# A decoder layer on one core: a seventh feed-forward unit computed during the page loads

## The chip, the cores and the metric

The kernel runs on one core of one Trainium2 chip. TensorE (PE) does the products, VectorE (DVE), ScalarE (ACT) and GpSimd (POOL) the elementwise work, and SyncE (SP) issues nearly all DMAs. The metric is the device time of one execution in microseconds, as the median of several runs.

## The reference, cut to what matters

One decoder layer, float32, for a prompt of 256 tokens and eight samples of one token each, with 2048 earlier tokens per sample in a paged cache.

```python
z = x @ w_in                                  # q, k, v, B, C, h
att = attend(q, k, v)                         # 8 heads x 64; samples: block-sparse over cached pages
conv_y, conv_buf_new = causal_dwconv(gc * h, conv_buf, w_conv)
mix = jnp.concatenate([att, gb * conv_y], axis=-1) @ w_out
x1 = layer_norm(DEEPNORM_ALPHA * x + mix, ln1_g, ln1_b)
up, ffn_buf_new = causal_dwconv(x1 @ w_up, ffn_buf, w_fconv)     # w_up: 1024 x 5632
a, g = jnp.split(up, 2, axis=-1)
f = (jax.nn.silu(a) * g) @ w_down                                # w_down: 2816 x 1024
y = layer_norm(DEEPNORM_ALPHA * x1 + f, ln2_g, ln2_b)
```

## The kernel before, in words

Activations stand transposed: channels on the 128 partitions, and 264 columns (256 prompt tokens, then 8 samples). The feed-forward width of 2816 is cut into 22 units. A unit is 128 columns of the `a` half and 128 of the `g` half of `w_up`: 1 MB of weights, eight steps over the 1024 channels for each half.

The work comes in stages. First the input projection (`z_tile`) while the keys of all pages are scanned on VectorE, GpSimd and ScalarE (`multiply`, `reduce`, `multiply_page`, `sum_products`). Then the values: 32 groups of four pages (1 MB each, four DMAs), `values(b, s)` with number v = 4b + s, loaded by SyncE into a ring of homes (`HOMES`); from group 9 on, group v takes the home of group v - 6 and its load waits for that one's use (`s_vused`). Sample b is done after group 4b + 3: VectorE masks it (`masked_values`), PE transposes it (`sample_outputs`), VectorE sums the columns (`sample_columns`).

The first E = 6 units are *early*. Their weights are loaded among the values and PE multiplies them with the 256 prompt columns of `x1T` in plain float32 (`early_part`, `early_half(u, a)`), each unit in PSUM bank u % 4, between value groups. Units 0 to 3 come in four "quads" (rows of 512 columns, loaded by `load_quad`), units 4 and 5 as a pair for each half (rows of 256 columns, `load_pair`, behind groups 24 and 31), into the first half of the ring `wring`. ScalarE takes an early unit out of PSUM (`early_scaled`), VectorE convolves it (`early_convolved`), ScalarE applies silu, VectorE multiplies the halves (`gated`) into `fe`.

Where PE would stand idle among the last groups, `keep_clock(bank, n)` issues a product whose result nobody reads. Behind group 31 PE does the samples' path: their rows of the mixer output, the layer norm, and then, once the samples' `x1` is there (`s_xsp`), the product of the samples with all early units' weights. For it the kernel uses strips of 32 PE columns, four at once: the two halves of two units form one group, and there are ES = 3 groups, each with its PSUM bank; ScalarE copies a group's result (`ev`), and PE transposes it. GpSimd splits `x1` meanwhile into a high and a low part.

Then the *late* units, NL = 16 of them: ScalarE rounds the weights to a high part (`up_high`), VectorE subtracts (`low`), and PE does three products per step over all 264 columns (`split_product`, high times high, high times low, low times high), alternating between two slots (`late_slot`) with two PSUM banks each. SyncE loads a late unit (`load_up`, two DMAs with rows of 128 columns) once the slot is free. The down product follows in the same manner, eight tiles of 22 steps (`down_tile`), then the second layer norm.

The orders in each engine's queue are written out by hand; engines meet at semaphores only. The query buffer `qk[:, 0]` (4096 columns) holds the broadcast queries until the key scan ends; its first half takes quad 0 after sample 3's keys, and `qk[:, 1]` holds products of the scan, and `fe` later. The last product of the key scan is well ahead of value group 20.

Of the kernel before, what the change touches and what calls it, by code (L numbers as in the profile page):

```python
# [22 lines left out]
P = 128  # L23
D = 1024
KT = D // P
# [23 lines left out]
E = 6  # L49
QUAD = 4  # L50
ES = E // 2
# [8 lines left out]
def build(nc, x_prompt, x_sample, cache_k, cache_v, state_conv, state_ffn_conv, page_table,  # L60
# [13 lines left out]
    with ctx:  # L74
# [98 lines left out]
        quads = [h.rearrange("p (k n) -> p k n", k=KT // 2) for h in quad_home]  # L173
        pairs = [wring[:, 0, a * UNIT:(a + 1) * UNIT].rearrange("p (k n) -> p k n", k=KT) for a in range(2)]

        def early(u, k, a):
            if u < QUAD:
                return quads[2 * a + k // 4][:, k % 4, u * P:(u + 1) * P]
            return pairs[a][:, k, (u - QUAD) * P:(u - QUAD + 1) * P]

        fe = qk[:, 1, 0:E * NPR].rearrange("p (u n) -> p u n", u=E)
# [23 lines left out]
                     (NS, ps[0:NS, 2:4, :], NPR, srows[0:NS, :]))  # L205
# [116 lines left out]
        def down_bank(m):  # L322
            return 7 if m == 0 else m % 2
# [14 lines left out]
        def _(sp):  # L338
# [77 lines left out]

            def load_pair(a):
                sp.wait_ge(s_mix, KT)
                first = a * FF + QUAD * P
                sp.dma_start(pairs[a], wup[:, :, first:first + 2 * P]).then_inc(s_eu[4 + a], 16)  # L420
# [45 lines left out]
            for b in range(3, NS):  # L466
                ids_v = page_ids(b)
                for s in range(SLOTS):
                    v = SLOTS * b + s
                    load_values(v, ids_v)  # L470
                    if v in (12, 13):
                        load_quad(v - 10)
                    elif v in (24, 31):
                        load_pair((24, 31).index(v))
# [162 lines left out]
        def _(act):  # L637
# [177 lines left out]
            def early_scaled(u):  # L815
                bank = ps[:, u % 4, :].rearrange("p (a n) -> p a n", a=2)
                act.wait_ge(s_u, QUAD + 1 + u if u < QUAD else 2 * QUAD + 3 + u - QUAD)
# [23 lines left out]
            for u in range(QUAD):  # L841
                early_scaled(u)
                silu(u)
# [4 lines left out]
            early_scaled(4)  # L848
            early_scaled(5)
            silu(4)  # L850
            silu(5)
            act.wait_ge(s_sr, 1)
            for i in range(ES):
                act.wait_ge(s_es, i + 1)
                nc.scalar.activation(ev[:, i, :], ps[:, (7, 4, 5, 6)[i], 0:P], ACT.Copy).then_inc(s_ec, 1)
# [44 lines left out]
        def _(dve):  # L900
# [305 lines left out]
            sample_columns(5)  # L1206
            masked_values(6)
            sample_columns(6)
# [30 lines left out]
            early_convolved(4)  # L1239
            early_convolved(5)  # L1240
            gated(4)
            gated(5)
            low(1, UNIT)
# [120 lines left out]
        def _(pe):  # L1364
# [329 lines left out]
            def early_part(u, a, first, end):  # L1694
                if first == 0:
                    if u == QUAD:
                        pe.wait_ge(s_eu[4 + a], 16)
                    elif u == 0:
                        pe.wait_ge(s_eu[2 * a], 16)
                    if a == 0 and u >= 4:  # L1700
                        pe.wait_ge(s_cv, 2 * (u - 4) + 2)
                        pe.wait_ge(s_tl, u - 3)
# [42 lines left out]
            value_range(21, 23)  # L1745
            sample_outputs(3)
            early_half(3, 1)
            value_range(23, 25)
            sample_outputs(4)
            early_half(4, 0)  # L1750
            value_range(25, 27)
            sample_outputs(5)
            early_half(5, 0)
            value_range(27, 30)
            sample_outputs(6)
            pe.wait_ge(s_cv, 2 * QUAD)
            pe.wait_ge(s_tl, QUAD)
            keep_clock(3, 448)
            value_range(30, 31)
            keep_clock(3, 512)  # L1760
            keep_clock(3, 384)
# [3 lines left out]
            early_part(4, 1, 0, 4)  # L1765
# [11 lines left out]
            early_part(4, 1, 4, KT)  # L1777
# [4 lines left out]
            early_half(5, 1)  # L1782
# [5 lines left out]
            for i in range(ES):  # L1788
                units = range(2 * i, 2 * i + 2)
# [7 lines left out]
            for i in range(ES):  # L1797
                pe.wait_ge(s_ec, i + 1)
                turn(ps[:, 7, i * P:(i + 1) * P], ev[:, i, :]).then_inc(s_et, 1)
# [129 lines left out]
```

## Time and profile before

| | |
|---|---|
| median of 3 runs | 447.43 us (447.05 to 448.56) |
| the profiled execution | 448.32 us |
| its span, first to last instruction | 446.5 us |
| PE busy | 416.1 us (93%), 2911 products |
| VectorE busy | 296.0 us (66%) |
| ScalarE busy | 181.6 us (41%) |
| GpSimd busy | 104.4 us (23%) |
| moved by DMA | 124.85 MB, mean 280 GB/s |
| chain that ended last | PE 55%, VectorE 18%, SyncE's queue 11%, issue 6%, DMA 5% |

The span is what the profile's times count from; the execution's own time has about 1.8 us more around it. Busy times of PE overlap from one product to the next, since products are pipelined: the time from start to start is what a product costs, and it is shorter than its duration. A float32 product appears as two instructions.

### The profile page before, as it was taken

How to read it: one execution, taken by the hardware profiler on the slowest of the kernel's cores; microseconds unless marked ns; L12 is line 12 of the kernel's file. 1: busy time of each engine (PE TensorE's matmuls, PEld its weight loads, DVE VectorE, ACT ScalarE, POOL GpSimd, SP SyncE). 2: the span in 40 equal slices, each digit the busy share in tenths (PEclk: the TensorE clock that was granted, in tenths of full speed). 3: DMA queues.
4: the chain of work that ended last, by engine and by line, in shares of the span. 5: the costliest groups of instructions: out<-in, count | busy, mean ns of one | idle time of the engine just before them, and what ended most of it. 6: DMA issues, size and time to landing. Idle time of an engine off the chain costs nothing.

```text
span 446.5 us, 8259 instructions
## 1 busy us (share of the span) xinstructions
PE 416.1 (93%) x2911; PEld 341.0 (76%) x2911; DVE 296.0 (66%) x383; ACT 181.6 (41%) x694; POOL 104.4 (23%) x133
## 2 busy tenths in 40 slices
PE   4999999999999998999798989999999999999990
PEld 4588887876866774664364369999999999999990
DVE  0496999999799976944351264766666877534536
ACT  1476568653377334011110043455554456224201
POOL 1003033995255231100000436211222221000002
PEclk9999999999999999999999999999999999999997
DMA  8999999999999999999999953566666685968002
GB/s 294 385 329 386 385 388 379 370 357 390 398 386 372 351 393 387 386 386 386 386 377 386 304 166 111 159 178 189 189 182 170 166 215 155 234 174 212 24 1 97
DMA packets 109515, 124.85 MB, mean 280 GB/s; under 512 B 5775, under 2 KB 66920, under 8 KB 109466
## 3 DMA queue, kind: packets, MB, share of 16 engines
q1 hardware_dynamic: 101138, 107.55, 72.5%
q10 hardware_dynamic: 8336, 16.78, 10.5%
q8 instruction: 23, 0.38, 0.4%
q14 instruction: 18, 0.15, 0.1%
HBM read 121.90 MB, written 2.61 MB: 279 GB/s over the span
## 4 chain that ended last, share of the span: by engine, by line
PE 55%; DVE 18%; SPq 11%; issue 6%; DMA 5%; POOL 2%; ACT 1%; DVEq 0%; POOLq 0%; ACTq 0%
PE ps L1815 11%; PE ps L1816 11%; PE ps L1817 11%; SPq L354 8%; DVE qk L930 5%; DVE T L940 5%; PE ps L1432 4%; PE ps L1627 4%; PE ps L1708 3%; PE ps L1603 3%; PE ps L1629 3%; PE ps L1372 3%; DMA wring<-in_cache_v 2%; DMA KV<-in_cache_k 2%; POOL x1l L605 1%
## 5 line engine op out<-in xcount | busy, mean ns | idle before, releaser
L1177 DVE TENSOR_TENSOR wlo<-KV,whi 128x2048 fp32r<-128x2048 f32 (+1 forms) x24 | 61.8, 2576 | 57.1 <-ACT whi L832 29.1
L1432 PE MATMUL ps<-xT,wring 128*128 128x264 f32 x384 | 89.6, 389 | 0.0
L1432 PEld LDWEIGHTS ps<-xT,wring 128*128 128x128 f32 x384 | 71.9, 191 | 13.4 <-issue 1.7
L1815 PE MATMUL ps<-x1h,whi 128*128 128x264 f32 x256 | 73.8, 288 | 0.2
L930 DVE TENSOR_TENSOR qk<-KV,qk 128x1536 f32<-128x1536 f32 (+1 forms) x32 | 67.8, 2122 | 9.2 <-DMA KV<-in_cache_k 5.5
L1817 PE MATMUL ps<-x1h,wlo 128*128 128x264 f32 x256 | 72.7, 284 | 0.0
L1816 PE MATMUL ps<-x1l,whi 128*128 128x264 f32 x256 | 72.7, 284 | 0.0
L662 ACT ACTIVATE qk<-qk 128x64 f32<-128x64 f32 x216 | 51.8, 244 | 28.5 <-POOL qk L553 21.1
L940 DVE TENSOR_REDUCE T<-qk 128x24 f32<-128x1536 f32 (+1 forms) x32 | 58.4, 1827 | 0.0
L1815 PE MATMUL ps<-fh,whi 128*128 128x264 f32 x176 | 50.4, 286 | 0.1
L1816 PE MATMUL ps<-fl,whi 128*128 128x264 f32 x176 | 50.0, 284 | 0.0
L1817 PE MATMUL ps<-fh,wlo 128*128 128x264 f32 x176 | 50.0, 284 | 0.0
L1815 PEld LDWEIGHTS ps<-x1h,whi 128*128 128x128 f32 x256 | 48.3, 189 | 1.6 <-issue 1.4
L1816 PEld LDWEIGHTS ps<-x1l,whi 128*128 128x128 f32 x256 | 48.3, 189 | 0.0
L1817 PEld LDWEIGHTS ps<-x1h,wlo 128*128 128x128 f32 x256 | 48.1, 188 | 0.0
L832 ACT ACTIVATE whi<-KV 128x2048 fp32r<-128x2048 f32 x16 | 30.6, 1915 | 42.3 <-PE ps L1817 42.3
L662 ACT ACTIVATION_READ_ACCUMULATOR qk<-qk 128x1 f32 x216 | 41.0, 190 | 0.0
L553 POOL TENSOR_TENSOR qk<-KV,qk 128x512 f32<-128x512 f32 x19 | 28.9, 1525 | 45.7 <-DMA KV<-in_cache_k 24.0
L1157 DVE SCALAR_TENSOR_TENSOR U<-ps,stT,U 128x255 f32<-128x255 f32 (+1 forms) x84 | 34.5, 474 | 0.0
L1815 PEld LDWEIGHTS ps<-fh,whi 128*128 128x128 f32 x176 | 33.2, 189 | 0.5 <-DVE wlo L1177 0.4
L1816 PEld LDWEIGHTS ps<-fl,whi 128*128 128x128 f32 x176 | 33.2, 189 | 0.0
L1817 PEld LDWEIGHTS ps<-fh,wlo 128*128 128x128 f32 x176 | 33.1, 188 | 0.0
(218 smaller groups left out, 578.9 us busy)
## 6 DMA issues: line engine op xcount, KB each, us to landing
KV<-in_cache_k SPq DMA_DIRECT2D x128, 256.0 KB, 7.3
KV<-in_w_ffn_up SPq DMA_DIRECT2D x32, 512.0 KB, 5.1
KV<-in_cache_v SPq DMA_DIRECT2D x60, 256.0 KB, 8.5
wring<-in_cache_v SPq DMA_DIRECT2D x56, 256.0 KB, 7.5
KV<-in_w_ffn_down SPq DMA_DIRECT2D x8, 1408.0 KB, 7.0
wring<-in_w_in ACTq DMA_DIRECT2D x5, 2048.0 KB, 15.1
zbuf<-in_cache_v SPq DMA_DIRECT2D x12, 256.0 KB, 6.0
zbuf<-in_w_ffn_up SPq DMA_DIRECT2D x3, 1024.0 KB, 11.5
```

Source lines behind the costliest of these rows:

```text
L354: sp.dma_start(dst[:, g, :], pages[bass.ds(ids[g], 1)].rearrange("o t d -> (o t) d")).then_inc(landed, 16)
L553: nc.gpsimd.tensor_tensor(prod[:, j % 2, GD * DA:GP * DA], kv[:, s, GD, :], qb[:, b, :], ALU.mult).then_inc(s_kpool, 1)
L662: ins = nc.scalar.activation(x, x, ACT.Copy, accum_out=T[:, b // 4, GP * s + GD, b % 4 * NH + h:b % 4 * NH + h + 1])
L832: nc.scalar.activation(whi[s][:, 0:UNIT], w2[s][:, 0:UNIT], ACT.Copy).then_inc(s_hi, 1)
L930: nc.vector.tensor_tensor(prod[:, j % 2, 0:n * DA].rearrange("p (g d) -> p g d", g=n), kv[:, s, 0:n], q, ALU.mult).then_inc(s_kused, 1)
L940: nc.vector.tensor_reduce(dst, prod[:, j % 2, 0:n * DA].rearrange("p (g h d) -> p g h d", h=NH, d=DH), AX.X, ALU.add).then_inc(s_red, 1)
L1157: nc.vector.scalar_tensor_tensor(out, bank[:, 0:n], tap(u + a * FT, k), out, ALU.mult, ALU.add)\
L1177: nc.vector.tensor_tensor(wlo[s][:, 0:n], w2[s][:, 0:n], whi[s][:, 0:n], ALU.subtract).then_inc(s_lo, 1)
L1432: ins = nc.tensor.matmul(ps[:, z_bank(n), 0:R], tile[k], xT[:, k, :], start=k == 0, stop=k == KT - 1)
L1815: nc.tensor.matmul(out, wh[k], xh[k], start=k == 0, stop=False)
L1816: nc.tensor.matmul(out, wh[k], xl[k], start=False, stop=False)
L1817: ins = nc.tensor.matmul(out, wl[k], xh[k], start=False, stop=k == n - 1)
```

## The change

E goes from 6 to 7, so there are 15 late units, and ES from 3 to 4 groups, of which the last holds one unit (two strips). The new fifth unit (u = 4, "solo") gets the second half of the query buffer. SyncE loads it behind value group 20 in two DMAs, with rows of 128 columns. The pairs, loaded where they were, now hold units 5 and 6. PE does both halves of unit 4 around value group 23, the first halves of 5 and 6 behind groups 25 and 26 to 27, and the second halves of 5 and 6 where those of 4 and 5 were. Of the four unread products (448, 512, 384 and 320 columns) those of 448 and 384 go. Convolution and gating of unit 4 go ahead in VectorE's and ScalarE's queues. As NL is odd now, the down product begins in the other slot, and its PSUM banks and those of the last rows change with it.

```diff
--- before.py
+++ after.py
@@ -46,9 +46,9 @@
 Z_ORDER = (0, 1, 4, 5, 2, 3)
 STATE_ROWS = 2 * NS
 STACK = STATE_ROWS + 3
-E = 6
+E = 7
 QUAD = 4
-ES = E // 2
+ES = (E + 1) // 2
 NL = FT - E
 WHOLE = (14, 16, 18, 20, 31)
 POOLED = (9, 10, 11, 12) + tuple(range(17, 32))
@@ -171,13 +171,17 @@
         UNIT = KT * 2 * P
         quad_home = [qk[:, 0, 0:UNIT], zbuf[:, UNIT:2 * UNIT], zbuf[:, 2 * UNIT:3 * UNIT], zbuf[:, 0:UNIT]]
         quads = [h.rearrange("p (k n) -> p k n", k=KT // 2) for h in quad_home]
+        solo = qk[:, 0, UNIT:2 * UNIT].rearrange("p (k a n) -> p k a n", k=KT, a=2)
         pairs = [wring[:, 0, a * UNIT:(a + 1) * UNIT].rearrange("p (k n) -> p k n", k=KT) for a in range(2)]
 
         def early(u, k, a):
             if u < QUAD:
                 return quads[2 * a + k // 4][:, k % 4, u * P:(u + 1) * P]
-            return pairs[a][:, k, (u - QUAD) * P:(u - QUAD + 1) * P]
-
+            if u == QUAD:
+                return solo[:, k, a, :]
+            return pairs[a][:, k, (u - QUAD - 1) * P:(u - QUAD) * P]
+
+        assert E * NPR <= 2 * UNIT - KT * R
         fe = qk[:, 1, 0:E * NPR].rearrange("p (u n) -> p u n", u=E)
         w2 = [KV[:, s * FT * P:(s + 1) * FT * P] for s in range(2)]
         U = at("U", hs_mem, [P, 2, 2, NPR], F32)
@@ -202,7 +206,7 @@
         ps = ctx.enter_context(nc.psum_tensor("ps", [P, 8, 512], F32))[:]
 
         row_tiles = ((P, ps[:, 4:6, :], 0, rows[:, 0, :]), (P, ps[:, 6:8, :], P, rows[:, 1, :]),
-                     (NS, ps[0:NS, 2:4, :], NPR, srows[0:NS, :]))
+                     (NS, ps[0:NS, 0:2, :], NPR, srows[0:NS, :]))
         first_rows = ((P, ps[:, 2:4, :], 0, rows[:, 0, :]), (P, ps[:, 0:2, :], P, rows[:, 1, :]),
                       (NS, ps[0:NS, 4:6, :], NPR, srows[0:NS, :]))
 
@@ -320,7 +324,7 @@
             return (0, 1, 4)[m % 3]
 
         def down_bank(m):
-            return 7 if m == 0 else m % 2
+            return 7 if m == 0 else 2 * late_slot(NL) + m % 2
 
         def act_sums(j):
             return sum(i not in WHOLE for i in range(j))
@@ -414,9 +418,15 @@
                     sp.wait_ge(s_vused, 7)
                 sp.dma_start(quads[i], wup[:, k:k + 4, a * FF:a * FF + QUAD * P]).then_inc(s_eu[i], 16)
 
+            def load_solo():
+                sp.wait_ge(s_kused, NS * SLOTS)
+                sp.wait_ge(s_kpool, pool_pages(NS * SLOTS))
+                for a in range(2):
+                    sp.dma_start(solo[:, :, a, :], wup[:, :, QUAD * P + a * FF:QUAD * P + a * FF + P]).then_inc(s_eu[6], 16)
+
             def load_pair(a):
                 sp.wait_ge(s_mix, KT)
-                first = a * FF + QUAD * P
+                first = a * FF + (QUAD + 1) * P
                 sp.dma_start(pairs[a], wup[:, :, first:first + 2 * P]).then_inc(s_eu[4 + a], 16)
 
             load_consts(0, 8)
@@ -470,6 +480,8 @@
                     load_values(v, ids_v)
                     if v in (12, 13):
                         load_quad(v - 10)
+                    elif v == 20:
+                        load_solo()
                     elif v in (24, 31):
                         load_pair((24, 31).index(v))
             sp.wait_ge(s_ctail, 1)
@@ -814,7 +826,7 @@
 
             def early_scaled(u):
                 bank = ps[:, u % 4, :].rearrange("p (a n) -> p a n", a=2)
-                act.wait_ge(s_u, QUAD + 1 + u if u < QUAD else 2 * QUAD + 3 + u - QUAD)
+                act.wait_ge(s_u, QUAD + 1 + u if u < QUAD else 2 * QUAD + 2 if u == QUAD else 2 * QUAD + 4 + u - QUAD)
                 if u >= 2:
                     act.wait_ge(s_f, u - 1)
                 for a in range(2):
@@ -838,21 +850,22 @@
 
             exponentials(1)
             nc.scalar.activation(idle, nhalf[:, 0:1], ACT.Silu)
-            for u in range(QUAD):
+            for u in range(QUAD + 1):
                 early_scaled(u)
                 silu(u)
             act.wait_ge(s_sw, 1)
             nc.scalar.activation(er[:, 0, :], ps[:, 6, :], ACT.Copy).then_inc(s_swc, 1)
             up_high(0)
             normalise(first_rows, 2, s_shift, 2, s_srx)
-            early_scaled(4)
             early_scaled(5)
-            silu(4)
+            early_scaled(6)
             silu(5)
+            silu(6)
             act.wait_ge(s_sr, 1)
             for i in range(ES):
                 act.wait_ge(s_es, i + 1)
-                nc.scalar.activation(ev[:, i, :], ps[:, (7, 4, 5, 6)[i], 0:P], ACT.Copy).then_inc(s_ec, 1)
+                n = P if 2 * i + 1 < E else P // 2
+                nc.scalar.activation(ev[0:n, i, :], ps[0:n, (7, 4, 5, 6)[i], 0:P], ACT.Copy).then_inc(s_ec, 1)
             up_high(1)
 
             def late_scaled(v):
@@ -1204,7 +1217,9 @@
             early_convolved(3)
             gated(3)
             sample_columns(5)
+            early_convolved(4)
             masked_values(6)
+            gated(4)
             sample_columns(6)
             masked_values(7)
             sample_columns(7)
@@ -1236,10 +1251,10 @@
             nc.vector.tensor_copy(x1h[:, :, NPR:R], new).then_inc(s_xsh, 1)
             dve.wait_ge(s_xsh, 1)
             nc.vector.tensor_tensor(x1l[:, :, NPR:R], new, x1h[:, :, NPR:R], ALU.subtract).then_inc(s_xsh, 1)
-            early_convolved(4)
             early_convolved(5)
-            gated(4)
+            early_convolved(6)
             gated(5)
+            gated(6)
             low(1, UNIT)
             dve.wait_ge(s_et, ES)
             tails = uptail[:, 2:NTAIL, :].rearrange("p r (a n) -> p a n r", a=2)
@@ -1694,6 +1709,8 @@
             def early_part(u, a, first, end):
                 if first == 0:
                     if u == QUAD:
+                        pe.wait_ge(s_eu[6], 32)
+                    elif u == QUAD + 1:
                         pe.wait_ge(s_eu[4 + a], 16)
                     elif u == 0:
                         pe.wait_ge(s_eu[2 * a], 16)
@@ -1742,27 +1759,32 @@
             sample_outputs(2)
             value_range(20, 21)
             early_half(2, 1)
-            value_range(21, 23)
+            value_range(21, 22)
+            early_half(3, 1)
+            value_range(22, 23)
             sample_outputs(3)
-            early_half(3, 1)
-            value_range(23, 25)
+            early_half(4, 0)
+            value_range(23, 24)
+            early_half(4, 1)
+            value_range(24, 25)
             sample_outputs(4)
-            early_half(4, 0)
-            value_range(25, 27)
+            value_range(25, 26)
+            early_half(5, 0)
+            value_range(26, 27)
             sample_outputs(5)
-            early_half(5, 0)
-            value_range(27, 30)
+            early_part(6, 0, 0, 4)
+            value_range(27, 28)
+            early_part(6, 0, 4, KT)
+            value_range(28, 30)
             sample_outputs(6)
+            value_range(30, 31)
             pe.wait_ge(s_cv, 2 * QUAD)
             pe.wait_ge(s_tl, QUAD)
-            keep_clock(3, 448)
-            value_range(30, 31)
             keep_clock(3, 512)
-            keep_clock(3, 384)
             value_range(31, 32)
             keep_clock(3, 320)
             sample_outputs(7)
-            early_part(4, 1, 0, 4)
+            early_part(5, 1, 0, 4)
             pe.wait_ge(s_xso, 1)
             pe.wait_ge(s_om, NS)
             for c in range(2):
@@ -1774,19 +1796,19 @@
                 ins = nc.tensor.matmul(ps[32 * g:32 * g + NS, 6 + m // 4, g * P:(g + 1) * P], rT[:, m, NPR:R], ident,
                                        start=False, stop=True)
             ins.then_inc(s_sw, 1)
-            early_part(4, 1, 4, KT)
+            early_part(5, 1, 4, KT)
             pe.wait_ge(s_swc, 2)
             for c in range(2):
                 ins = nc.tensor.matmul(ps[0:NS, 4 + c, :], sel, er[:, c, :], start=True, stop=True)
             ins.then_inc(s_sr, 1)
-            early_half(5, 1)
+            early_half(6, 1)
             pe.wait_ge(s_srx, 1)
             for m in range(KT):
                 ins = turn(ps[:, 6, 256 + m * NS:256 + (m + 1) * NS], srows[0:NS, m * P:(m + 1) * P], NS)
             ins.then_inc(s_sb, 1)
             pe.wait_ge(s_xsp, 1)
             for i in range(ES):
-                units = range(2 * i, 2 * i + 2)
+                units = range(2 * i, min(2 * i + 2, E))
                 for k in range(KT):
                     for u in units:
                         for a in range(2):
@@ -1796,7 +1818,8 @@
                 ins.then_inc(s_es, 1)
             for i in range(ES):
                 pe.wait_ge(s_ec, i + 1)
-                turn(ps[:, 7, i * P:(i + 1) * P], ev[:, i, :]).then_inc(s_et, 1)
+                n = P if 2 * i + 1 < E else P // 2
+                turn(ps[:, 7, i * P:i * P + n], ev[0:n, i, :], n).then_inc(s_et, 1)
 
             def split_product(out, wh, wl, xh, xl, prompt=None, between=None):
                 n = len(wh)
```

## Rows read from the trace of the kernel before

**Rows 1.** The page: three rows of the span in 40 slices.

```profile
PE   4999999999999998999798989999999999999990
...
DMA  8999999999999999999999953566666685968002
GB/s 294 385 329 386 385 388 379 370 357 390 398 386 372 351 393 387 386 386 386 386 377 386 304 166 111 159 178 189 189 182 170 166 215 155 234 174 212 24 1 97
```

**Rows 2.** Windows: engines' busy time (instructions), granted clock, DMA share, GB/s.

```profile
243.00:245.00 2.00, 0.92 (x8) 0.16 (x8) 0.00 (x0) 0.00 (x0) 0.00 (x0) 1.00 1.05 386
...
251.00:253.00 2.00, 1.38 (x8) 0.79 (x7) 1.22 (x3) 0.00 (x0) 1.84 (x4) 1.00 1.06 274
```

**Rows 3.** Timeline of PE, 216 to 253 us: start, duration, instruction, idle before.

```profile
216.81 1.07 PE L1603 MATMUL ps<-KV,Pw 128*32 128x512 f32 x8 [1.83 <-DMA KV<-in_cache_v]
217.81 3.72 PE L1708 MATMUL ps<-catT,zbuf 128*128 128x256 f32 x16
221.46 1.07 PE L1603 MATMUL ps<-KV,Pw 128*32 128x512 f32 x8
222.34 1.04 PE L1603 MATMUL ps<-wring,Pw 128*32 128x512 f32 x8
223.31 0.66 PE L1372 MATMUL ps<-ident,OM 128*128 128x128 f32 x4
223.81 3.62 PE L1708 MATMUL ps<-catT,zbuf 128*128 128x256 f32 x16
227.36 1.07 PE L1603 MATMUL ps<-KV,Pw 128*32 128x512 f32 x8
...
246.79 1.07 PE L1603 MATMUL ps<-wring,Pw 128*32 128x512 f32 x8 [0.30 <-DMA wring<-in_cache_v]
247.79 1.77 PE L1645 MATMUL ps<-diag,ident 128*128 128x512 f32 x4
249.53 1.06 PE L1603 MATMUL ps<-KV,Pw 128*32 128x512 f32 x8
...
251.41 0.66 PE L1372 MATMUL ps<-ident,OM 128*128 128x128 f32 x4
252.61 2.00 PE L1708 MATMUL ps<-catT,wring 128*128 128x256 f32 x8 [0.54 <-DMA wring<-in_w_ffn_up]
```

**Rows 4.** Timeline of SyncE's queue: the issue of value group 30.

```profile
235.24 2.19 SPq L354 DMA_DIRECT2D wring<-in_cache_v  x4
```

**Rows 5.** Chain of waits, and timeline of PE: the samples' up product.

```profile
266.05 5.45 PE ps L1794 x192
...
266.05 0.30 PE L1794 MATMUL ps<-qk,xsP 128*32 128x128 f32 x1 [0.94 <-DVE xsP L1235]
266.06 0.30 PE L1794 MATMUL ps<-zbuf,xsP 128*32 128x128 f32 x1
...
266.19 0.27 PE L1794 MATMUL ps<-qk,xsP 128*32 128x128 f32 x1
```

**Rows 6.** Chain of waits: late units 0 and 14; and a window over all 16.

```profile
272.23 0.35 PE ps L1815
...
355.68 0.35 PE ps L1815
...
272.20:367.30 95.10, 94.93 (x768) 93.60 (x768) 65.70 (x92) 48.25 (x91) 23.63 (x39) 1.00 0.64 175
```

**Rows 7.** Windows: one late unit's load each, and one half microsecond.

```profile
278.00:281.00 3.00, 3.00 (x28) 3.00 (x27) 0.76 (x1) 2.70 (x5) 2.51 (x5) 1.00 1.08 300
...
290.00:293.00 3.00, 3.00 (x27) 3.00 (x26) 1.11 (x2) 2.83 (x6) 0.00 (x0) 1.00 1.10 307
...
291.50:292.00 0.50, 0.50 (x7) 0.50 (x6) 0.00 (x0) 0.50 (x2) 0.00 (x0) 1.00 1.15 346
```

**Rows 8.** Timeline of VectorE: convolution and gating of early unit 3.

```profile
230.51 1.64 DVE L1157 SCALAR_TENSOR_TENSOR U<-ps,stT,U 128x255 f32<-128x255 f32 x4
232.26 0.43 DVE L1172 TENSOR_TENSOR qk<-U 128x256 f32<-128x256 f32 x1
```

## The prediction

> **What bounds the kernel now.** I read the page first, for which resource is full where. The slices of the span [rows 1] show two regimes. Up to the 24th slice (about 257 us) DMA is at 9 tenths and moves some 386 GB/s; after it TensorE (PE) is at 9 tenths in every slice and DMA is not. So a microsecond of PE work costs one only behind about 250 us, and a megabyte costs time only before it. The change takes an FFN unit out of the second regime and puts it into the first.
>
> Next the stretches of the span by window [rows 2], to see whether the first regime is full to its end. It is: at 243 us the share of the DMA engines is 1.05, with 386 GB/s, the level of the slices before. The order of PE's work between 216 and 253 us [rows 3] shows that PE follows the transfers: value groups 20 and 30, and behind them the half on the second pair, each start behind an idle time that a DMA ends. From the start of group 20 (216.81) to that of group 30 (246.79) eleven megabytes land (groups 21 to 30 and one pair): 29.98 / 11 = 2.73 us each. SyncE's issues [rows 4] run far ahead of that: group 30 is issued at 235.24 and used 11.55 us later, so its queue always has work.
>
> Then the chain of waits for the two stretches behind: the sample rows' up product of the early units [rows 5] and the late units [rows 6]. The chain enters the first late unit at 272.23 and the fifteenth at 355.68, 14 units on: 83.45 / 14 = 5.96 us each, and there PE has no gap to speak of (94.93 us busy of 95.10). The granted clock is 1.00 (2.4 GHz) in every stretch read.
>
> **The change part by part.**
>
> *One late unit fewer.* It removes 48 products of the split kind: 5.96 us of PE, all on the path. The transition to the down product is reached by the same orders in every queue; slots and PSUM banks only swap parity. **-5.96 us.** ScalarE, VectorE and GpSimd lose or move their share of that unit, which PE hides.
>
> *The load of the solo unit.* 1 MB more before the end of the value phase, two DMAs behind group 20. SyncE does not wait for it: group 14 already needed the same count of used keys. Its two issues stand in a queue that is 11.55 us ahead. The price is transfer time, since DMA is full. At the rate of the other megabytes it is 2.73 us. But this one has rows of 128 columns, as the late units' loads have, and these are slower [rows 7]: a late load fills the engines (share 1.08 and 1.10) at 300 and 307 GB/s, its best half microsecond is 346. 1.05 MB at 307 is 3.4 us. The lower bound is 2.73; the upper is 3.8, from the 274 GB/s of 251 to 253 us, where such a load goes beside other things [rows 2]. The late loads are the same kind, so I take **3.4 us**. The Trainium skill (DMA: Bandwidth & Descriptors, Specifications) says that transfers reach line rate from 512 bytes on, which is the length of these rows. By that rule the load would take the 2.73 us. The trace does not agree: 307 against 386 GB/s; the rule's result is a rival below.
>
> *PE's products in the value phase.* Two halves are added (before: two single halves of 4 and 5; after: both of 4, one each of 5 and 6), two unread products go. From [rows 3]: a half takes 3.65 us (217.81 to 221.46), later ones 3.55, say 3.6; a value group 0.95 (1.00, 0.88, 0.97); four transposes 0.5. Does PE still reach group 31 in time? In the new queue, group 21 lands at 216.8 + 3.4 + 2.7 = 222.9 and PE waits for it. Behind that, ahead of group 31, stand ten groups (9.5), five halves (18.0), four sets of transposes (2.0) and the one unread product left (0.9: half of the row of 1.77 for two): 30.4 us, so 253.3. Group 31 lands at about 246.8 + 2.7 + 3.4 = 252.9. PE is thus level with the transfers, 0.4 us behind: group 31 starts at 253.3, 3.8 us later than the 249.53 of before. Next late is the half that uses the second pair: the old one waited 0.54 us for its load and began at 252.61; the new one is released by the load at 252.61 + 3.4 = 256.0, or by PE at 251.9 + 3.8 = 255.7. So the load decides, and **what follows shifts by 3.4 us**, 3.3 to 3.8 as the two trade places. PE's lateness can also reach the loads, since group v + 6 waits for the home of v. The narrowest: group 24 is used by 237.9, and SyncE would issue group 30 at 235.24 + 3.4 = 238.6. Even a miss of some microseconds is covered by the 11 us that are in the queue.
>
> *VectorE and ScalarE.* Convolution and gating of unit 4 (1.64 + 0.43 us [rows 8]) move ahead of masked_values(6) and sample_columns(6); behind them wait sample_outputs(6), value group 30's successors and the tail. The fifth sample's transposes end near 244.4, its column sum at 245.1, the convolution at 246.8; the mask waits for group 27 (about 247.1) and is done at 247.9, and PE wants it at 250.9. Three microseconds of cover, so nothing; without cover it would be 2.1 us at most. The tail keeps two units (5, 6 for 4, 5) and is as long as before.
>
> *The sample rows' product.* Three groups of two units take 5.45 us, 1.82 each [rows 5]. The new fourth holds one unit, so two column strips of PE instead of four. Within a group the four strips start together (266.05, 266.06) and the next four instructions follow a pass later (266.19), and so on, so a strip's own pass sets the time and half a group costs a whole one: **+1.8 us**; if it were set by the count of instructions, 0.9, the lower bound. Above 1.82 nothing points. The copy of its result and the transposes behind it follow the last group as before, and nothing new is exposed.
>
> **Sum:** -5.96 + 3.4 + 1.8 = -0.76 us. On the profiled execution: span 446.5 to 445.7, time 448.32 to 447.6. The median of the runs is 447.43, 0.9 below the profiled one, so I predict 447.43 - 0.76 = **446.7 us**. What a measurement can tell from no change is 0.3% or 1.34 us.
>
> **Rivals.**
>
> *A. The solo load goes at full rate.* Then it costs 2.73 us, but PE takes over as the bound: group 21 lands 0.7 earlier, PE reaches the half of the second pair at 255.0, against a load at 255.3, a shift of 2.7 to 3.1. That gives 2.9 + 1.8 - 5.96 = -1.3: 446.2 us, on the edge of faster. For it: half microseconds of 346 GB/s, and a queue that is never empty hides the ramps of a lone load. Against: 307 over a whole load at a share above the value phase's. The skill's rule named above would make this the outcome.
>
> *B. The fourth sample group costs half.* 3.4 + 0.9 - 5.96 = -1.7: 445.8 us, faster. With A as well it would be -2.2, 445.3. Against it: the even pace of the groups of four strips.
>
> *C. TensorE becomes the bound (the other side).* The place is the run of five halves ahead of group 31. The sum leaves PE 0.4 us behind the load. Every further microsecond there, by a wait of unit 6's first half for its bank or of sample_outputs(6) for the mask, goes one for one into the tail once the pair's load is passed (0.3 us). The change is level when the shift reaches 4.16 us (5.96 - 1.8), PE then 0.7 us later than summed; slower by 0.3% from 5.5 us on, PE 2.1 us later than summed. A VectorE chain that misses its 3 us of cover by 2 would do: 447.43 + 1.5 = 448.9 us. For it: only 0.9 us of unread products is left as cushion, and VectorE's queue has more in it; against: every wait that I followed has microseconds of room.
>
> *D. No net change of any kind,* the load at 3.8 us: 3.8 + 1.8 - 5.96 = -0.4, 447.1 us.
>
> **How the numbers follow.** The forecast (load 3.2 to 3.6, fourth group 1.8) 0.45; A 0.15; B 0.12, with or without A; C 0.13, about a quarter of it short of the 0.3% bound; D 0.15. Faster by over 0.3%: B, and half of A, and a little of the forecast by the scatter of medians (the runs of before span 447.05 to 448.56): 0.23. Slower: C's greater part and a trace of D: 0.12. Same: 0.65. The range: down to 445.6, B's value with some scatter; up to 448.2, between no change and C's 448.9, which leaves out about 0.1 on each side.
>
> **What the profile after should show.** The late units still 5.96 us apart, 15 of them; the first one entered at 272.23 + 3.4 + 1.8 = 277.4 us. The sample product at 7.2 to 7.3 us instead of 5.45, starting at 269.4. DMA's share still 1.05 to 1.1 through 250 us, with some 3 us of it at 300 to 340 GB/s between 217 and 224 us. Group 31 at 253 to 253.5 us with little or no idle time of PE in the ten groups before it; the solo's first half not waiting for its load. The mask of the seventh sample before 249 us. The prediction is wrong if the shift at the half of the second pair is under 2.9 or over 4 us, if the fourth sample group takes under 1.6 us, or if PE waits for VectorE between 244 and 252 us.

## The result, and the profile after

The kernel after takes **449.33 us** (median of 13 runs, 448.35 to 451.36) against 447.67 us for the kernel before beside it (13 runs): a ratio of 1.0034, 95% interval 1.002 to 1.0048. It is slower. The forecast was 446.7 us, with a range of 445.6 to 448.2.

The profiled execution took 448.92 us with a span of 447.1 us, 0.6 us over that of before. The page has the same two regimes as [rows 1]:

```profile
PE 418.0 (93%) x2924; PEld 341.5 (76%) x2924; DVE 294.5 (66%) x382; ACT 179.8 (40%) x693; POOL 104.7 (23%) x133
...
PE   5999998999999998998799997999999999999990
...
DMA  8999999999999999999999963366666685968002
...
q8 instruction: 23, 0.38, 0.4%
```

The last row played no part in the prediction: a DMA queue that carries instructions. In 23 packets it moves 16 KB each, in the kernel before too, and PE has 5,848 instruction records (2924 of products and as many of weight loads), one packet for some 254 of them. That the queue is PE's is inferred: the other engines have under 700 records each.

The chain of waits, from the samples' up product into the late units (start, duration, what), answers to [rows 5] and [rows 6]:

```profile
269.25 5.23 PE ps L1816 x184
274.48 1.64 issue
276.13 2.16 PE ps L1816 x40
278.29 0.68 PE ps L1387 x4
...
278.98 0.36 PE ps L1838
...
350.51 0.36 PE ps L1838
```

The product starts at 269.25, as expected (269.4). Then, after 184 of its 224 product records, PE stops for 1.64 us. The row says "issue": no semaphore and no transfer that the profile ties to an instruction. The first late unit starts at 278.98, 9.73 us behind the product's start; before it was 6.16 us by the timeline. The late units are 5.96 us apart as before (278.98 to 350.51, 12 units). So the block costs 3.57 us more, where 1.8 were in the sum.

The timeline of PE in the value phase (start, duration, instruction, idle before) answers to [rows 3]:

```profile
212.63 1.06 PE L1618 MATMUL ps<-KV,Pw 128*32 128x512 f32 x8 [1.44 <-DMA KV<-in_cache_v]
...
215.48 1.07 PE L1618 MATMUL ps<-KV,Pw 128*32 128x512 f32 x8 [1.19 <-DMA KV<-in_cache_v]
216.48 3.72 PE L1725 MATMUL ps<-catT,zbuf 128*128 128x256 f32 x16
221.91 1.06 PE L1618 MATMUL ps<-KV,Pw 128*32 128x512 f32 x8 [1.72 <-DMA KV<-in_cache_v]
...
252.14 1.13 PE L1660 MATMUL ps<-diag,ident 128*128 128x512 f32 x2
253.20 1.06 PE L1618 MATMUL ps<-KV,Pw 128*32 128x512 f32 x8
...
255.81 1.99 PE L1725 MATMUL ps<-catT,wring 128*128 128x256 f32 x8
```

The rows are groups 19, 20, the half between, 21, the one unread product, group 31 and the half on the second pair. Group 21 is the last that PE waits for; from 221.91 on its queue is full, and group 31 starts at 253.20 (forecast 253.3). The half on the second pair starts 3.20 us later than before; counted from group 19, the last one that the solo load can't touch, 43.18 us against 39.28 (252.61 - 213.33, a start that the trace of before gives), 3.9 us later. VectorE's mask of the seventh sample is done before 248 us, with the room that was forecast.

### The profile page after: what moved, and what is told of

It is laid out like the page before. It is cut to its first block, busy times and chain, and to the rows that moved or that the text cites. A ratio compares the mean times of both kernels' runs of the same rounds, so it can differ in the third digit from the quotient of the medians.

```text
span 447.1 us, 8281 instructions
## 1 busy us (share of the span) xinstructions
PE 418.0 (93%) x2924; PEld 341.5 (76%) x2924; DVE 294.5 (66%) x382; ACT 179.8 (40%) x693; POOL 104.7 (23%) x133
## 4 chain that ended last, share of the span: by engine, by line
PE 58%; DVE 18%; SPq 10%; issue 6%; DMA 4%; POOL 2%; ACT 1%; DVEq 0%; POOLq 0%; ACTq 0%
PE ps L1838 11%; PE ps L1839 10%; PE ps L1840 10%; PE ps L1725 6%; SPq L358 5%; DVE qk L943 5%; DVE T L953 5%; PE ps L1618 5%; PE ps L1447 4%; PE ps L1642 3%; PE ps L1644 3%; PE ps L1387 3%; DMA KV<-in_cache_k 2%; PE ps L1816 2%; POOL x1l L617 1%
## 5 line engine op out<-in xcount | busy, mean ns | idle before, releaser
L1190 DVE TENSOR_TENSOR wlo<-KV,whi 128x2048 fp32r<-128x2048 f32 (+1 forms) x23 | 59.5, 2588 | 58.7 <-ACT whi L844 31.0
L1838 PE MATMUL ps<-x1h,whi 128*128 128x264 f32 x240 | 68.9, 287 | 0.4
L1839 PE MATMUL ps<-x1l,whi 128*128 128x264 f32 x240 | 68.0, 283 | 0.0
L1840 PE MATMUL ps<-x1h,wlo 128*128 128x264 f32 x240 | 68.0, 283 | 0.0
L1838 PEld LDWEIGHTS ps<-x1h,whi 128*128 128x128 f32 x240 | 45.2, 188 | 1.7 <-issue 1.6
L1839 PEld LDWEIGHTS ps<-x1l,whi 128*128 128x128 f32 x240 | 45.3, 189 | 0.0
L1840 PEld LDWEIGHTS ps<-x1h,wlo 128*128 128x128 f32 x240 | 45.0, 188 | 0.0
L844 ACT ACTIVATE whi<-KV 128x2048 fp32r<-128x2048 f32 x15 | 28.7, 1915 | 39.5 <-PE ps L1840 39.5
L565 POOL TENSOR_TENSOR qk<-KV,qk 128x512 f32<-128x512 f32 x19 | 27.3, 1442 | 45.8 <-DMA KV<-in_cache_k 22.7
```

Of the source, the lines that this page charges most:

```text
L565: nc.gpsimd.tensor_tensor(prod[:, j % 2, GD * DA:GP * DA], kv[:, s, GD, :], qb[:, b, :], ALU.mult).then_inc(s_kpool, 1)
L844: nc.scalar.activation(whi[s][:, 0:UNIT], w2[s][:, 0:UNIT], ACT.Copy).then_inc(s_hi, 1)
L1190: nc.vector.tensor_tensor(wlo[s][:, 0:n], w2[s][:, 0:n], whi[s][:, 0:n], ALU.subtract).then_inc(s_lo, 1)
L1838: nc.tensor.matmul(out, wh[k], xh[k], start=k == 0, stop=False)
L1839: nc.tensor.matmul(out, wh[k], xl[k], start=False, stop=False)
L1840: ins = nc.tensor.matmul(out, wl[k], xh[k], start=False, stop=k == n - 1)
```

## The experiments

Three theories of the gap were put to the test. **I**: PE's instructions come in blocks by DMA, and where a block edge falls in the dense sample product decides. **C**: the block comes late because its transfer stands behind another load. **L**: the product is simply too long now. The windows show the other load. In the kernel after, the load of late unit 2 fills the engines until 274 us; the queues' rows of 271 to 273 us, and of 273 to 275 us, are

```profile
q1 hardware_dynamic: 1273, 0.64, 112.3%
```

```profile
q1 hardware_dynamic: 242, 0.12, 24.5%
q8 instruction: 1, 0.02, 3.7%
```

so the 16 KB go when the 1 MB is nearly through (at 273.58, 4.33 us into the product), and PE goes on at 276.13.

The kernel before has the same late packet: it too goes 4.33 us into the product, at 270.38, and PE does not stop there. What differs is the count of instructions ahead of the product. These rows of windows, from the span's start to the product's, are those of the kernel before, of the kernel after and of run 1 below; the third column is PE's busy time and its product records, each with a weight load beside it:

```profile
0.00:266.04 266.04, 246.56 (x1386) 1.00 1.02 365
0.00:269.24 269.24, 252.76 (x1414) 1.00 1.02 365
0.00:265.93 265.93, 249.32 (x1414) 0.99 1.02 365
```

The change puts 28 product records, so 56 instructions, ahead of the product: 64 for the two halves of one more unit, less 8 for the two dropped unread products. Run 1 puts the same 56 into the kernel before.

**1. The kernel before with 56 instructions more** ahead of the product, where PE waits for a transfer anyway.

```diff
+            def tiny(count):
+                pe.wait_ge(s_cv, 2)
+                pe.wait_ge(s_tl, 1)
+                for i in range(count):
+                    nc.tensor.matmul(ps[0:32, 0, 0:1], ident[:, 0:32], diag[:, 0:1], start=True, stop=True)
...
+            tiny(14)
             value_range(20, 21)
```

> The kernel before, with 14 one-column products that nobody reads (56 instructions of PE) in front of value group 20, where PE waits 1.83 us for a transfer anyway. Theory I (instruction blocks): PE's instructions arrive in blocks by DMA, and the 1.64 us gap of the kernel after lies where a block came late in the dense sample product; what matters is where the block edge falls, and 56 more instructions put it here as in the kernel after. Then a gap of about 1.3 to 1.7 us appears at instruction 350 or so of the sample product or just behind it, the first late unit starts at 273.5 to 274, and the time goes up by 1.3 to 1.7 us, to about 449.2. Theory L (length): the gap comes because the product has 224 instead of 192 instruction pairs. Then nothing changes: first late unit 6.2 us behind the product's start, time within 0.4 us of before. Theory N (the seventh unit itself: its buffer, its strips) also says no change.

Measured: 450.03 us against 447.46, ratio 1.0053 (1.0034 to 1.0073), more than the 1.3 to 1.7 us expected. The timeline of PE in the sample product:

```profile
270.33 0.84 PE L1801 MATMUL ps<-wring,xsP 128*32 128x128 f32 x24
272.79 0.43 PE L1801 MATMUL ps<-wring,xsP 128*32 128x128 f32 x8 [1.62 <-issue]
273.15 0.80 PE L1372 MATMUL ps<-ident,ev 128*128 128x128 f32 x3
273.93 0.36 PE L1822 MATMUL ps<-x1h,whi 128*128 128x264 f32 x1
```

Nothing of the change is in this kernel, and the gap is there, 1.62 us, behind the 184th product record as in the kernel after. Group 31 starts within 0.1 us of where it did (249.48). Theory L and the seventh unit as such fall. From the product's start to the first late unit it is 7.99 us, 1.83 more than before. The rest of the 2.6 us fits another cause: this profile has a stretch at half clock near 73 us, of which below, and five of the seven executions have a mean granted clock of 0.987 or 0.988 as it does; the other two took 449.04 and 449.84 us.

**2. and 3. The kernel after with 128 and with 64 instructions more**, half in front of group 20 and half in front of group 21. The edit is shown for 128; for 64 it has `tiny(8)` twice.

```diff
+            tiny(16)
             value_range(20, 21)
             early_half(2, 1)
+            tiny(16)
             value_range(21, 22)
```

> The kernel after, with 16 unread one-column products in front of value group 20 and 16 in front of group 21 (128 instructions of PE), where PE idles 1.19 and 1.72 us. Theory I: the block edge moves from inside the sample product to ahead of it, where PE's instructions are slow; the gap shrinks from 1.64 to under 0.6 us and the time falls by 1 to 2 us, to 447.3 to 448.3. Theory L and N: the gap stays at 1.6 us, time within 0.4 us of the kernel after (449.3).

> As the run with 128 instructions, but with 64 (8 and 8 products). Theory I: the block edge is still among the last instructions ahead of the product or its first, and the next block is needed inside it: the gap stays, 1.4 to 2 us, a little earlier in the product (near instruction 285 rather than 349). Theory L: the gap stays where it is. So together with the run with 128 it tells a place in the stream from a mere count of instructions added.

Measured: with 128, 447.60 us, ratio to before 1.0002 (0.9985 to 1.0018), no gap, first late unit 7.87 us behind the product's start. With 64, 448.78 us, ratio 1.0025 (1.0009 to 1.0041), a gap of 0.75 us, at 5.10 us into the product where it was at 6.88 us in the kernel after (the instruction behind the gap):

```profile
273.73 0.30 PE L1824 MATMUL ps<-wring,xsP 128*32 128x128 f32 x1 [0.75 <-issue]
```

The gap moves earlier and shrinks with more instructions put in front. With 64 it stands behind the 151st product record in place of the 184th, 66 instructions earlier (33 products and as many weight loads). I had expected 64 not to shrink it; the direction of the place was right, the size not. The trace shows why it shrank: the packet went 2.57 us into the product here, while the load of late unit 2 was still running. In all four profiles with a gap (the kernel after here and in run 10, runs 1 and 3) PE goes on 2.5 to 2.6 us behind the packet's start.

**4. The kernel after with the load of late unit 2 held** until the sample product is complete.

```diff
             for v in range(2, NL):
                 sp.wait_ge(s_lo, v - 1)
+                if v == 2:
+                    sp.wait_ge(s_es, ES)
                 load_up(v)
```

> The kernel after, with the load of late unit 2 held until the sample product is complete; unit 2 is not needed until 12 us later. Theory C (contention): the instruction block waits behind this load's packets, as its own transfer begins 4.3 us after the product's start in both traces, near the end of the load. Then the gap goes to under 0.5 us, and the time to 447.6 or so. If the block is late only for its position (theory I without contention) the gap stays at 1.6 us and the time at 449.3. If the load is held too long, the high part of unit 2 is late and PE waits there; expected 0.

Measured: 447.60 us against 447.46, ratio 0.9991 (0.9973 to 1.0009). The instruction stream of PE is that of the kernel after; the gap is gone. Its chain, and the queues' rows of 271 to 273 us:

```profile
269.86 7.18 PE ps L1818 x224
277.04 0.68 PE ps L1389 x4
277.73 0.36 PE ps L1840
```

```profile
q8 instruction: 1, 0.02, 3.0%
```

The packet now goes at 271.5, 1.7 us into the product, not 4.3.

**5. and 6. The kernel before with the hold**, with and without the 56 instructions.

> The kernel before with the 56 instructions of unread products, and the load of late unit 2 held until the sample product is complete. Theory I+C: the gap needs both, a block edge that falls badly and a load that the block's transfer stands behind. With the load held, the block's transfer begins some 1.7 us after the product's start instead of 4.3, the gap of 1.62 us goes, and the time is back within 0.4 us of before. Rival (position alone; the hold only helped the kernel after by chance): gap 1.6 us and 449.5 to 450.

> The kernel before with only the hold of that load. There is no gap in its trace, so the hold has nothing to remove: theory I+C says no change (within 0.4 us). Rival: the hold pays for another reason, for instance less traffic beside the sample product; then it gains 1 us or more here too, and its gain in the kernel after says nothing of instruction blocks.

Measured, against 447.17 us: 448.08 us with both (ratio 1.001, 0.9995 to 1.0026) and no gap, 6.16 us from the product's start to the first late unit as in the kernel before; 447.87 us with the hold alone (1.0017, 0.9999 to 1.0035). So the hold takes away what the 56 instructions cost, and gains nothing where there is no gap. The gap needs both: the edge in the wrong place and the load ahead of the block.

**7. The hold, and a half moved ahead of group 21**, into the wait of 1.72 us.

```diff
-            value_range(21, 22)
             early_half(3, 1)
+            value_range(21, 22)
```

> The kernel after with the hold, and the second half of early unit 3 moved ahead of value group 21, where PE waited 1.72 us for the transfer that the solo load had delayed. Theory T (the transfers bound the tail): PE reaches group 31 1.7 us earlier, finds it not landed, and the tail moves by 0.2 to 0.5 us only. Theory P (PE bounds the tail, its queue being full from group 21 on): the tail moves by 1 us or more, to under 446.8 us.

Measured: 447.61 us, ratio 1.0013 (0.999 to 1.0035), no gain that six runs can tell. Its trace has PE wait 0.59 us for group 31 (starting at 252.05) and 1.11 us for the second pair (255.69): the transfers bind. From group 19 to that half it is 42.75 us, 3.47 more than before. So theory T holds. The 3.47 us are the price of the solo load where nothing else binds; 3.4 was forecast.

**8. and 9. The hold, and the solo buffer from rows of 512 columns**, twice. The same 1 MB comes in longer rows, but they are other weights: these two kernels leave out the right values of unit 4 and serve for the time alone.

```diff
-                for a in range(2):
-                    sp.dma_start(solo[:, :, a, :], wup[:, :, QUAD * P + a * FF:QUAD * P + a * FF + P]).then_inc(s_eu[6], 16)
+                flat = qk[:, 0, UNIT:2 * UNIT].rearrange("p (k n) -> p k n", k=4)
+                for a in range(2):
+                    sp.dma_start(flat[:, 2 * a:2 * a + 2, :], wup[:, 2 * a:2 * a + 2, 0:512]).then_inc(s_eu[6], 16)
```

> The kernel after with the hold, and the solo buffer filled from rows of 512 columns (2 KB) in place of 128 (512 bytes), the same 1 MB; it holds other weights, so unit 4's values are not the reference's. Theory R (row length): group 21 lands 5.5 us behind group 20 instead of 6.3 or so, and the tail comes 0.6 to 0.9 us earlier, near 446.9. If row length does not matter for the time, as the rule of 512 bytes says, nothing changes (within 0.3 us).

> The solo buffer from rows of 2 KB once more. Its trace showed group 21 landing 8.80 us behind group 19, against 8.88 with the rows of 512 bytes: no gain; its median was 1.9 us lower. If the trace is right, the median comes within 0.5 us of the kernel with the held load beside it. If the median is right, it is again 1 us or more below.

Measured: ratios to before of 0.9974 (0.9953 to 0.9996) and 0.9978 (0.996 to 0.9997), against 0.9991 and 1.0001 for the hold alone: about 0.9 us, though the intervals overlap. From group 19 to group 21 the two traces have 8.80 and 8.10 us, those of the hold alone 8.88 and 8.85. Counted from group 20, which the solo load stands right behind, both show it: 5.31 and 5.18 us to group 21, against 5.96 and 5.90 with the hold alone and 6.43 in the kernel after. (Group 20 itself came 0.6 us later in run 8 than in the others, which hides it from group 19 on.) So long rows land some 0.7 us sooner at this place; that the whole kernel gains as much is likely by the times, not shown.

**10. and 11. The kernel after and the one with the hold once more**, beside each other.

> The kernel after once more, for its distribution and a second profile beside the same runs of before as the next three. Theory I+C: the gap is in this profile too, 1.5 to 1.9 us, at the same instruction of the sample product; time 1.2 to 1.8 us above before.

> The kernel after with the held load once more, to settle the size: the sum of the other terms (5.96 saved, 3.4 and 1.8 paid) says 0.8 us faster than before, 446.6 to 447; if the first measurement (level with before) stands, the paid terms come to 6 us rather than 5.2. Against the kernel after 1.5 to 2 us faster.

Measured, against 448.17 us: after 449.86 us, ratio 1.004 (1.002 to 1.006), with a gap of 1.74 us at the same instruction; with the hold 447.64 us, 1.0001 (0.9982 to 1.002), level again and not the 0.8 us faster that was expected. The profile of the first also shows the following around group 21, first the timeline of PE, then the windows (the third column from the right is the granted clock):

```profile
222.84 1.57 PE L1618 MATMUL ps<-KV,Pw 128*32 128x512 f32 x8 [1.98 <-DMA KV<-in_cache_v]
224.34 4.00 PE L1725 MATMUL ps<-catT,zbuf 128*128 128x256 f32 x12
```

```profile
221.00:223.00 2.00, 0.16 (x4) 0.16 (x8) 0.00 (x0) 0.80 (x3) 0.00 (x0) 1.00 1.04 376
223.00:225.00 2.00, 2.00 (x10) 0.57 (x3) 0.00 (x0) 0.00 (x0) 0.00 (x0) 0.57 1.05 392
225.00:227.00 2.00, 2.00 (x7) 1.62 (x6) 0.00 (x0) 0.00 (x0) 0.00 (x0) 0.58 1.04 385
```

Behind the wait for group 21, 1.98 us here, the clock falls to 1.2 GHz for about 3.4 us. As PE has no slack from there on, it arrives late: from group 19 to the sample product 58.28 us, in the first profile of the same kernel 56.62. Of these 1.7 us, 0.4 lie ahead of group 21, which came later itself; 1.3 lie behind it (48.64 us to the product against 47.34). It is in one profile of two.

**12. The hold, and one of eight steps of the fourth sample group**, so the kernel leaves out most of unit 6 for the samples.

```diff
-                for k in range(KT):
+                steps = KT if i < 3 else 1
+                for k in range(steps):
```

> The kernel after with the held load, and one of eight steps of the fourth sample group (unit 6's products with the samples over 128 of the 1024 channels only). Theory S (a strip's pass sets the pace, so half a group costs a whole one): the sample product is shorter by 7/8 of 1.82 = 1.6 us, and the time falls by as much, to 1.6 us below the run with the held load. Rival (the count of instructions sets it): 0.8 us.

Measured: ratio 0.9962 (0.9941 to 0.9982), 1.7 us below the hold alone; product and transposes 6.34 us instead of 7.87, so 1.5 us less where 1.6 was expected by theory S and 0.8 by its rival. Theory S holds.

**13. and 14. Versions meant to be kept**: the hold, with the fourth group on all four strips, and the same with the half moved as in 7. The edit is shown without the hold and without the wider copy and transpose of the group.

```diff
-                            g = 32 * (2 * (u % 2) + a)
+                            g = 32 * (2 * ((u if i < 3 else k) % 2) + a)
                             ins = nc.tensor.matmul(ps[g:g + 32, (7, 4, 5, 6)[i], 0:P], xsP[:, k, :], early(u, k, a),
-                                                   start=k == 0, stop=k == KT - 1)
+                                                   start=k < (1 if i < 3 else 2), stop=k >= (KT - 1 if i < 3 else KT - 2))
...
+            chain(ins)
+            for a in range(2):
+                src = ps[:, 7, :].rearrange("p (n a x) -> p a n x", a=2, x=32)
+                ins = nc.vector.tensor_tensor(tails[:, a, E - 1:E, :], tails[:, a, E - 1:E, :], src[:, a, E:E + 1, 0:NS], ALU.add)
             ins.then_inc(s_ett, 1)
```

> The kernel after with the held load, and the fourth sample group spread over all four strips: unit 6's even steps on strips 0 and 1, odd steps on strips 2 and 3, the two halves added on the way out. Theory S (a strip's pass sets the pace): the group takes 0.9 instead of 1.8 us, the sample product with its transposes 7.0 instead of 7.87, and the time is 0.9 us below the kernel with the held load: 446.6 to 447, 0.2 to 0.3% under before. Rival (instructions set the pace): 7.87 stays and the time is level with before.

> The same with the second half of early unit 3 ahead of value group 21, as in the earlier run, whose trace had PE wait for group 31 and the second pair instead (transfers bind there): nothing more than 0.3 us under the run beside it. If the gap between the spans (0.6 to 0.9 us below before) and the medians (level) comes from PE's full queue among the groups, which a stretch at half clock then hits in full, this one with its spare 0.6 and 1.1 us of PE should be 0.5 us better in the mean.

Measured: 447.33 us, ratio 0.9982 (0.9964 to 0.9999), and 446.32 us, ratio **0.9965** (0.9951 to 0.998). The chain of the first:

```profile
268.83 6.32 PE ps L1822 x224
275.15 0.72 PE ps L1393 x4
275.88 0.35 PE ps L1844
```

Product and transposes take 7.05 us instead of 7.87, as expected; the time is 0.3 us above the 446.6 to 447 expected. The second is faster than both kernels of this study: 0.35% under before. That it is also faster than the first (0.9982) the overlapping intervals do not show.

## Why the prediction was wrong

**The step that failed** is the last of *The sample rows' product*: "Above 1.82 nothing points", and "nothing new is exposed". The group itself costs what was said: with the gap away, product and transposes are 7.87 us, 1.71 over 6.16 (forecast 1.8). What the step put at nothing is a wait for PE's own instructions, 1.64 and 1.74 us in the two profiles; with it the block is 9.73 and 9.82 us long, 1.9 us over 7.87. This is the densest stretch of the kernel: 224 product records and as many weight loads in 7.2 us, so the 254 instructions of a block last some 4.1 us there against 15 us in the late units (two in 0.12 us). The gap needs two things. One is the place of the block's edge: the change puts 56 more instructions ahead of the product, and run 1 shows that these 56 alone bring the gap, at the same record, without the seventh unit and its longer product. The other is that the block's transfer goes late beside the load of late unit 2, which SyncE issues as soon as `low(0)` is done, 0.65 us ahead of the product, in both kernels. Runs 2, 4 and 5 take away one of the two each, the edge's place (2) or the load (4, 5), and the gap goes. Whether the longer product would have met an edge without the shift was not run. Why PE goes on only some 1.4 us after the packet's end stays open as well.

The Trainium skill (Runtime: NRT & Kernel Launch, Instruction fetch mechanics) describes this fetch, in blocks of 16 KiB by a DMA queue of the sequencer, and calls its cost mostly hidden; the block size agrees with the 23 packets here, the "hidden" does not, with 1.64 us on the path.

**Late unit, -5.96:** right; 5.96 from unit to unit again.

**Solo load, +3.4:** right, 3.47 where only the transfers bind. The row that was used for it (307 GB/s for rows of 128 columns) decided well against the 2.73 us of the full rate. Rival A did not come about. The landing of group 21 behind group 20 says the same by another row: 6.43 us for two megabytes where the full rate would give 5.5, and 5.2 to 5.3 once the rows were long.

**PE's products in the value phase:** right in the sum (group 31 at 253.20, forecast 253.3) and in the verdict that PE and the transfers are level. In the profile the half on the second pair came 3.9 us later counted from group 19, just above the 3.3 to 3.8 given (counted from the span's start 3.20, just below); with the hold the sample product is 3.4 and 3.5 us later counted in the same way. The 1.72 us wait at group 21 was in my sum ("PE waits for it"), but not what it can do: in one profile of two the clock fell behind it, and 1.3 us were lost.

**VectorE and ScalarE, 0:** right; the mask is done 2.9 us ahead of its use.

**The sum.** Counted from group 19, the traces give -5.96 + 3.90 + 3.57 = +1.5 us for the kernel after, and the medians are 1.66 us apart. Without the gap the three terms are -5.96 + 3.4 + 1.7 = -0.9, and the spans of the two profiles with the hold (445.9, 445.6) are 0.6 and 0.9 under the 446.5 of before. The timed runs give ratios of 0.9991 and 1.0001, that is -0.4 and 0.0 us, each within about 0.8. So the forecast of -0.76 for these terms is neither confirmed nor excluded by the times. The order of the kernels after in the times is what it should be: 1.0034 and 1.004 with the gap, 1.0025 with 0.75 us of it, 1.0002, 0.9991 and 1.0001 without. The change from after to the hold is 1.8 us by the times (mean of the two pairs of ratios), and 1.86 and 1.95 us in the length of the block.

**Of the rivals** none was this one. B had the group at half cost and fell. C, the slower one, put the loss among the five halves; its place was wrong, though the fall of the clock behind group 21 works through it. Its figures were also off by the prediction's own terms: with PE at the half at 255.7, the change is level when PE is 1.1 us later than summed (not 0.7) and 0.3% slower when it is 2.4 later (not 2.1), and missing by 2 us gives 448.4 (not 448.9).

**The clock's share** is small. Every execution has its mean granted clock on record; the five profiles at 0.988 or 0.989 all have a stretch of 3.4 us at half clock ahead of the end (of the two at 0.990, one has). At 0.989 or below are 6 of the 25 executions of the kernel after and 19 of the 98 of the kernel before that were timed beside the runs, about as large a share. Without them the medians of run 10 are 449.68 and 447.85 us, still 1.8 apart. Where the stretch lies in the executions that were not profiled stays open, and so does what the wait at group 21 costs by it: run 14 without the wait has the lowest ratio (0.9965 against 0.9982) and one such execution of 12 against three in run 13, but the same move gained nothing in run 7.

## What to carry to other kernels

Count instructions, not only time: where many short ones follow each other, look up when the last block of them was fetched (the packets of the instruction queue), and what large load was issued just ahead; a load that is not urgent can wait until the dense stretch is over. An unexplained "issue" gap in such a stretch is tested cheaply by a few unread instructions further up: if it moves by as many instructions, the fetch is the suspect, and holding the load beside it is the second test.

## What of the hardware was not expected

A fetch of instructions shares the DMA engines with the loads and can be held up by them: the packet went 4.3 us into the product with a 1 MB load in front, in three kernels, and 1.7 to 1.9 us without it (2.5 in run 6, whose block edge lies later). It need not wait for the load's end: in run 3 it went at 2.57 us, with the load running until some 4.5. The 56 unread instructions made the block 1.83 us longer, and with the load held 0.00.

The granted clock fell to 1.2 GHz for about 3.4 us behind waits of PE of 1.8 to 2.2 us in six profiles: at group 21 in run 10, and near 71 to 72 us in runs 1, 8, 9, 12 and 14. The length of the wait does not settle it: 1.83 us at group 20 in [rows 3], 1.86 us near 69 us in run 6 and 2.00 us at group 21 in run 12 were followed by no such fall. Near 72 us it is seen as an 8 in the clock's slices on the page of run 1:

```profile
PEclk9999998999999999999999999999999999999996
```

Two strips of PE columns take as long as four: one unit's group took 1.7 us, two units' 1.8, and the one unit spread over four strips 0.9.
